# Expert loop with the down products of the former expert among gate and up, and one stretch of half-block turns

## The reference, cut to what matters

```
def expert_choice_ffn(h, router_w, w_gate, w_up, w_down):     # 16 experts, D = 1024, F = 2048, fp32
    cap = EC_CAPACITY * n // N_EXPERTS                        # 2 * 512 // 16 = 64 rows of a trunk
    aff = softmax(xf @ router_w); gate, idx = top_k(aff.T, cap)
    xs = xf[idx]
    hid = silu(xs @ w_gate[e]) * (xs @ w_up[e])               # (64, 2048)
    out = (hid @ w_down[e]) * gate[..., None]                 # (64, 1024)
    y = zeros.at[idx].add(out)
```

## Time and profile before

| | |
|---|---|
| Median of three runs | 1569.38 us (1569.37 to 1569.9) |
| Profiled execution, its time | 1570.46 us |
| Span from its first to its last instruction | 1568.7 us |
| Mean granted TensorE clock | 0.998 of full speed |
| PE busy | 1556.5 us, 99% |
| DVE busy | 1294.0 us, 82% |
| ACT busy | 1044.9 us, 67% |
| DMA from 700 to 1400 us | mean 386 GB/s |

### The profile page before, as it was taken

One profiled execution on the slowest core, in us unless ns is written; L12 is line 12 of the kernel. 1 busy time (PEld: TensorE's weight loads), 2 busy tenths in 40 slices (PEclk: granted clock), 3 DMA queues, 4 the chain that ended last, 5 costly groups with the idle time before them and its releaser, 6 DMA issues.

```text
span 1568.7 us, 22519 instructions
## 1 busy us (share of the span) xinstructions
PE 1556.5 (99%) x8254; PEld 1264.1 (81%) x8254; DVE 1294.0 (82%) x1367; ACT 1044.9 (67%) x980; POOL 160.1 (10%) x72
## 2 busy tenths in 40 slices
PE   9999999999999999999999999999999999999997
PEld 7888878888864888888888888888888888888885
DVE  7684786684864889989899998989989898998987
ACT  6453555453453777777777777777777777777776
POOL 0000000000011020211101021020202102020112
PEclk9999999999999999999999999999999999999999
DMA  9543447333465999999999999999999999999998
GB/s 338 189 145 110 142 158 259 95 122 121 155 261 219 404 399 400 392 379 388 375 389 396 379 389 379 393 378 387 395 381 389 370 398 383 389 392 379 392 358 343
DMA packets 155395, 498.41 MB, mean 318 GB/s; under 512 B 9936, under 2 KB 35664, under 8 KB 155344
## 3 DMA queue, kind: packets, MB, share of 16 engines
q1 hardware_dynamic: 144624, 461.54, 76.7%
q0 software_dynamic: 8272, 30.94, 6.2%
q10 hardware_dynamic: 2448, 5.25, 1.2%
HBM read 473.57 MB, written 20.97 MB: 315 GB/s over the span
## 4 chain that ended last, share of the span: by engine, by line
PE 96%; DVE 1%; DMA 1%; ACT 1%; SPq 0%; issue 0%; POOLq 0%; DVEq 0%
PE ps L1787 80%; PE ps L1835 4%; PE ps L1842 2%; PE ps L1926 2%; PE ps L2284 2%; PE ps L1884 1%; PE ps L1895 1%; PE ps L2090 1%; PE ps L2236 1%; PE ps L2089 1%; DMA raw<-w_qkv 1%; PE ps L2342 0%; PE ps L2085 0%; PE ps L2107 0%; DVE arena L1245 0%
## 5 line engine op out<-in xcount | busy, mean ns | idle before, releaser
L1171 DVE TENSOR_TENSOR w_rest<-raw,w_high 128x2048 fp32r<-128x2048 f32 x212 | 505.2, 2407 | 66.2 <-ACT w_high L1073 49.1
L1073 ACT CAST w_high<-raw 128x2048 fp32r<-128x2048 f32 x184 | 352.5, 1916 | 133.2 <-PE ps L1787 132.1
L1787 PE MATMUL ps<-w_high,xt_high 128*128 128x512 f32 x984 | 307.2, 392 | 0.0
L1787 PE MATMUL ps<-w_high,xt_rest 128*128 128x512 f32 x984 | 304.3, 389 | 0.0
L1787 PE MATMUL ps<-w_rest,xt_high 128*128 128x512 f32 x984 | 304.3, 389 | 0.0
L1171 DVE TENSOR_TENSOR w_rest<-raw_more,w_high 128x2048 fp32r<-128x2048 f32 x92 | 209.3, 2287 | 38.4 <-ACT w_high L1073 38.3
L1073 ACT CAST w_high<-raw_more 128x2048 fp32r<-128x2048 f32 x92 | 176.3, 1917 | 59.4 <-PE ps L1787 57.7
L1787 PEld LDWEIGHTS ps<-w_high,xt_rest 128*128 128x128 f32 x984 | 184.7, 188 | 38.5
L1787 PEld LDWEIGHTS ps<-w_rest,xt_high 128*128 128x128 f32 x984 | 184.8, 188 | 38.5
L1171 DVE TENSOR_TENSOR w_rest<-early,w_high 128x2048 fp32r<-128x2048 f32 x90 | 203.5, 2284 | 13.9 <-ACT w_high L1073 13.9
L1073 ACT CAST w_high<-early 128x2048 fp32r<-128x2048 f32 x90 | 172.5, 1917 | 59.1 <-PE ps L1787 59.1
(11 more groups left out here) (284 smaller groups left out, 1932.5 us busy)
## 6 DMA issues: line engine op xcount, KB each, us to landing
raw<-w_down SPq DMA_DIRECT2D x64, 1024.0 KB, 7.5
raw<-w_gate SPq DMA_DIRECT2D x62, 1024.0 KB, 7.4
raw<-w_up SPq DMA_DIRECT2D x62, 1024.0 KB, 7.6
raw_more<-w_down SPq DMA_DIRECT2D x32, 1024.0 KB, 7.1
early<-w_down SPq DMA_DIRECT2D x32, 1024.0 KB, 7.5
raw_more<-w_gate SPq DMA_DIRECT2D x31, 1024.0 KB
raw_more<-w_up SPq DMA_DIRECT2D x31, 1024.0 KB, 9.3
early<-w_gate SPq DMA_DIRECT2D x31, 1024.0 KB, 8.3
```

Source lines behind the costliest of these rows:

```text
L1073: nc.scalar.copy(w_high[:, i % SLOTS, :], src).then_inc(high_done, 1)
L1171: nc.vector.tensor_tensor(w_rest[:, j, :], src, w_high[:, j, :].bitcast(F32), ALU.subtract).then_inc(rest_done, 1)
L1787: done = nc.tensor.matmul(out, lhs, rhs, start=start and part == 0, stop=stop and part == 2)
```

## The change

**The loop is skewed by a whole expert.** While PE makes gate and up of expert f + 1, the down pairs of expert f stand among them. One round of the loop (f from 1 to 13) is now: gate and up, first half (pairs 8 to 15 of the round), one down pair (16), gate and up, second half (17 to 24), three down pairs (25 to 27), all three turns, then the four down pairs of the second hidden half (28 to 31). The last four continue the numbering of the next round: pair 32 is its pair 8. Expert 0 and the last two experts have their own orders, the last expert that of before.

**The turns are in half blocks.** Each 128x128 transpose becomes two, of the lower and the upper 64 rows, into the two banks of a pair of banks. A stretch is 48 transposes without a matmul between them. The rows go to banks 0 and 1, the first hidden half to 2 and 3, the second to 6 and 7: six banks. Two of these pairs belong to gate and up, so the first two pairs after the stretch wait for DVE (`xtr_done`, `htr_done`), and the second half of gate and up waits for silu and its product (`silu_done`, `hid_done`), since only one down pair lies between the halves.

**Buffers.** The two hidden halves get their own `silu` or `hid` buffer, multiplied in place (`acts`), and their own turned block: `odd_high` and `odd_rest` are new, 8 KB a partition. The copies out of PSUM read runs of 64 columns from two banks in turn (`turned`) and write in one run.

**POOL** now gathers the rows right after the turn of the former rows, and scatters a result after that.

```
+        odd_high, odd_rest = sb_line("odd_high", [P, D], F32R), sb_line("odd_rest", [P, D], F32R)
+        def turned(banks):
+            return bank(banks, 2).rearrange("p (r c t) -> p c r t", r=2, t=HD)
+        acts = (silu, hid)
+        ht = ((ht_high, ht_rest), (odd_high, odd_rest))
...
-                nc.scalar.copy(xt_high[:, :], bank(6, 2)).then_inc(xth_done, 1)
+                nc.scalar.copy(by_halves(xt_high), turned(banks)).then_inc(xth_done, 1)
...
-            def rest_of_expert(e):
-                rows_high(e + 1)
-                highs(e, 12, 12 + HT_AFTER)
-                hidden_high(2 * e + 1)
...
+            with act.Fori(1, E - 2) as f:
+                highs(f, 12, 19)
+                step_silu(2 * f + 2, pairs_before(f) + 16, 0)
+                highs(f, 19, 28)
+                step_silu(2 * f + 3, pairs_before(f) + 25, 1)
+                highs(f, 28, 31)
+                rows_high(f + 2)
+                highs(f, 31, 32)
+                hidden_high(2 * f + 2, 0, 2)
+                highs(f, 32, 36)
+                hidden_high(2 * f + 3, 1, 6, pairs_before(f) + 32)
+                result(f, pairs_before(f) + 32)
...
+            with dve.Fori(1, E - 2) as f:
+                rests(f, 12, 19)
+                step_hidden(2 * f + 2, 0)
+                rests(f, 19, 28)
+                step_hidden(2 * f + 3, 1)
+                rests(f, 28, 31)
+                rows_rest(f + 2)
+                rests(f, 31, 32)
+                hidden_rest(2 * f + 2, 0, 2)
+                rests(f, 32, 36)
+                hidden_rest(2 * f + 3, 1)
...
-                    last = nc.tensor.transpose(bank(6, 2)[:, kc * P:(kc + 1) * P], xg[:, kc * P:(kc + 1) * P], ident[:, :])
+            def turn_by_halves(c, src, banks=6):
+                for r in range(2):
+                    on = slice(r * HD, (r + 1) * HD)
+                    last = nc.tensor.transpose(bank(banks + r)[:, c * HD:(c + 1) * HD], src[on, c * P:(c + 1) * P], ident[on, on])
+                return last
+            def all_turns(e):
+                pe.wait_ge(rows_scaled, e + 1)
+                pe.wait_ge(hid_done, 2 * e + 2)
+                pe.wait_ge(htr_done, 2 * e)
+                if not isinstance(e, int):
+                    pe.nop(nofuse=True)
+                rows_t(0)
+                hidden_t(acts[0], 2)
+                hidden_t(acts[1], 6)
...
-            def rest_of_expert(e):
-                at = lambda s: lambda i: body_q(e, s + i)
-                rows_t(e + 1, 2 * e + 1)
-                pe.wait_ge(ys_done, e + 1)
-                down(2 * e, 0, at(0), 8)
-                pe.wait_ge(xtr_done, e + 3)
-                hidden_t(2 * e + 1)
-                gate_up(2 * e + 2, at(12))
-                down(2 * e + 1, 1, at(0), 20)
-                hidden_t(2 * e + 2)
+            with pe.Fori(1, E - 2) as f:
+                gate_up(f, 8, (xtr_done, f + 3), (htr_done, 2 * f + 1))
+                pe.wait_ge(ys_done, f + 1)
+                down(2 * f, 0, f, 16, 0, 1)
+                gate_up(f, 17, (silu_done, 2 * f + 3), (hid_done, 2 * f + 3))
+                down(2 * f, 0, f, 24, 1, 4)
+                all_turns(f + 1)
+                down(2 * f + 1, 1, f, 28)
```

More of the change, by code:

```diff
@@ L591, in _, with load_run @@
                 load_bias(b, GROUPS, 1)
-            def load_run(e, i, rows_of, of, h, count):
-                for jj in range(count):
+            def load_run(e, i, rows_of, of, h, end, first=0):
+                for jj in range(first, end):
                     load_pair(e, i + jj, rows_of(of, h, jj))
@@ L692, in _, with next_rows @@
             pool.wait_ge(route_done, TRUNKS)
-            for e in range(E - 1):
+            def next_rows(e):
                 pool.wait_ge(xt_mm, 2 * (e + 1))
@@ L706, in _ @@
                                         compute_op=ALU.add).then_inc(scattered, 16)
+            next_rows(0)
+            next_rows(1)
+            for e in range(2, E - 1):
+                next_rows(e)
+                scatter(e - 2)
+            scatter(E - 3)
+            scatter(E - 2)
             pool.wait_ge(rows_scaled, E - 1)
@@ L1036, in step_silu, with rows_high @@
                     return
-                nc.scalar.activation(silu, bank(0, 2), ACT.Silu).then_inc(silu_done, 1)
-            def rows_high(e):
+                nc.scalar.activation(acts[odd], bank(0, 2), ACT.Silu).then_inc(silu_done, 1)
+            def rows_high(e, banks=0):
                 if isinstance(e, int) and e == 0:
@@ L1044, in rows_high, with hidden_high @@
                 act.wait_ge(xt_mm, 2 * (e + 1))
[L1045 to L1047 removed]
+                nc.scalar.copy(by_halves(xt_high), turned(banks)).then_inc(xth_done, 1)
+            def hidden_high(s, odd, banks=6, used_by_down=None):
                 act.wait_ge(ht_mm, s + 1)
[L1049 removed]
+                if used_by_down is not None:
+                    act.wait_ge(pair_used, used_by_down)
+                nc.scalar.copy(by_halves(ht[odd][0]), turned(banks)).then_inc(hth_done, 1)
             def result(e, used_by_down):
@@ L2249, in gate_up, with down @@
                     last.then_inc(pair_used, 1)
-            def down(s, h, q_of, lo, first=0, end=D_PAIRS, lhs=(ht_high, ht_rest)):
+            def down(s, h, e, lo, first=0, end=D_PAIRS, lhs=None):
+                lhs = lhs or ht[h]
                 pe.wait_ge(htr_done, s + 1)
@@ L2272, in fourth, with hidden_t, first_hidden_t @@
                 last.then_inc(pair_used, 1)
-            def hidden_t(s, lo=0, hi=HALF // P):
-                if not isinstance(s, int):
-                    pe.wait_ge(hid_done, s + 1)
-                elif s == 0:
-                    pe.wait_ge(half_hid if lo == 0 else hid_done, 1)
-                    pe.wait_ge(third_hid_done, 1)
+            def hidden_t(src, banks=6):
+                for c in range(HALF // P):
+                    last = turn_by_halves(c, src, banks)
+                last.then_inc(ht_mm, 1)
+            def first_hidden_t(s, lo=0, hi=HALF // P):
+                pe.wait_ge(third_hid_done, 1)
+                if s == 0 and lo == 0:
+                    pe.wait_ge(half_hid, 1)
                 else:
@@ L2323, in _ @@
[L2323 to L2333 removed]
+            pe.wait_ge(rows_scaled, 1)
@@ new lines, in _ @@
+            gate_up(E - 2, 8, (xtr_done, E + 1), (htr_done, 2 * E - 3))
+            pe.wait_ge(ys_done, E - 1)
+            down(2 * E - 4, 0, E - 2, 16)
+            pe.wait_ge(hid_done, 2 * E - 1)
+            pe.wait_ge(htr_done, 2 * E - 2)
+            hidden_t(acts[0])
+            down(2 * E - 3, 1, E - 2, 20)
+            gate_up(E - 1, 0)
+            pe.wait_ge(ys_done, E)
+            down(2 * E - 2, 0, E - 1, 8, 0, 2)
+            pe.wait_ge(hid_done, 2 * E)
+            for c in range(HALF // P):
+                last = turn_whole(c, acts[1])
@@ L2334, in _ @@
+            last.then_inc(ht_mm, 1)
+            down(2 * E - 2, 0, E - 1, 8, 2, 4)
+            down(2 * E - 1, 1, E - 1, 12, 0, 2, lhs=(xt_high, xt_rest))
             pe.wait_ge(whole_done, 1)
```

170 lines of the change are left out of this document (102 added, 68 removed).

## The result

The changed kernel takes 1558.6 us (median of four runs, 1558.19 to 1558.78) against 1569.59 for the one before beside it: a ratio of 0.9928, 95% interval 0.9916 to 0.9941. That is 11.0 us less; 1558.5 had been predicted. The profiled execution took 1558.77 us with a span of 1557.0, 11.7 less than the span before.

A forecast was written before the change was run, and what follows sets the result against it. PE's own instructions were taken to bound the kernel. Fourteen stretches saving 0.78 us each give 10.9, with waits and lone turns at nothing: 1569.38 - 10.9 = 1558.5 us, range 1556.5 to 1565.

The forecast's parts named there:

- The bound: Whole loop: PE is never idle and waits for nobody, so only shortening PE's own instructions can help.
- The price of a stretch: Three turns as 48 half blocks in one stretch: 48 x 0.032 + 0.32 = 1.86 us, against 2.64 before.
- The gain: Stretches of turns, one before the loop and 13 in it: 0.78 us saved each, 14 x 0.78 = 10.9 us.
- The turns left alone: Rows of expert 1, hidden halves of experts 0 and 14: -0.05 us each, first hidden half about +0.1; together nothing.
- First rival: Last 16 transposes of a stretch come at 0.070 us, not 0.032: 1567.0 us; chance 0.10 in some degree.
- Second rival: Loads become the bound, unable to give the 1.2% more an expert wants: nothing gained, 1569.4 us; chance 0.05.
- Third rival: DVE's copies behind a stretch take 2.4 us, not 1.2; pair 12 stalls 2.1 us: 1587.9; chance 0.07 in some degree.

## Why the prediction was right

- **The bound.** That only PE's own instructions count is shown by both sides: the skewed order with whole blocks has the time of before, though every wait, buffer and bank in it is new, and the doubled rests cost nothing as long as POOL leaves DVE room for them.
- **The price of a stretch.** Predicted 1.86 us, measured 1.83. I had split one row of 32 into pace and fixed part by the length shown for it, 0.032 and 0.32. The lengths of 16, 48 and 96 give 0.031 and 0.34 to 0.37 without that. The two small errors go in opposite directions; for 48 blocks they nearly cancel.
- **The gain.** 0.78 us a round predicted, 0.82 measured, 14 times. The span fell by 11.7, the medians by 11.0, where 10.9 was predicted. That the median hits the forecast to 0.1 us is luck: the runs of one kernel differ by 0.5 to 0.6.
- **The turns left alone** were costed at 0.83 and measure 0.85 (the last of them, from 1490.35 to 1492.11, less 0.91), as the stretches of 16 in two experiments do. The half-block turn in the old order, 1 us in all instead of 2.3, is where this shows.
- **First rival, a slower pace beyond 32.** False: 96 come as 32 do. So the two figures of the Trainium skill (page TensorE: Matmul & The Clock Gate) that I had weighed for it, the queue of 64 in its table of the engine and the 62 ns where firmware decodes (section "Wait — 56ns, not 53.3ns?"), set no pace here: the 96 blocks took 31 ns each, weight loads included.
- **Second rival, the loads.** False: the round is 1.2% shorter and in the loop none of PE, DVE and ACT waits for a load of weights; from 700 to 1400 us they move 390 GB/s.
- **Third rival, dearer copies.** The copies cost what plain ones do. Its mechanism is real: doubled rests stall PE at pair 12, the place named, and a little at pair 9, which I had not named. Its size was off: I had 1.5 us of margin and a stall of 2.1, the run shows 2.1 and 1.2. POOL's multiply came 7.4 us behind the stretch and not 10, since its gather took 1.5 us to issue and not 2.8 and the data then came 1.5 us sooner. So it fell on the rest of pair 9 and not on those of 10 and 11, and held DVE up by 2.0, not 1.8; DVE swallowed a part of the doubled copies in idle time.
- **Wrong in detail.** I took a one-sided block at 0.070 us from a row of eight and concluded that two sides overlap to less than half of it. A long one-sided stretch takes 0.063, two sides in turn 0.031: 48 blocks of one side and 96 of two take the same 3.19 us. And the expectation of 1585 for one side first was wrong because I had thought the overlap needs neighbours; it reaches over some three blocks at each change of side.

Where the gain comes from, then: two halves on one side cost 0.126 us, a whole block 0.109, two halves on two sides 0.062. The overlap alone makes half blocks cheaper, by 8 x 0.047 = 0.38 us a turn, and the 0.34 to 0.37 us of entering and leaving it eat that unless three turns share them. Where these 0.35 us fall can be read from PE's starts around a stretch of the changed kernel: the first block comes 0.54 us after the last two matmuls and not 0.45 (0.09 more), the first matmul behind comes 1.63 us after the first block and not 48 x 0.031 = 1.49 (0.14 more), and its successor but one after 0.57 and not 0.45 (0.12 more). Why PE takes this time at the change between the two kinds isn't shown.

## What to carry to other kernels

Read a mode's price at two lengths, as a fixed part and a pace: here the fixed part (about 0.35 us) was as large as what one turn could win, so the same transposes gained 1 us in 45 places and 11 us in 14. When work is regrouped to share such a part, the price is paid in waits elsewhere; list for each the time at which it is wanted and the time at which it is ready, and look which other engine's work falls into the gap (here POOL's multiply, whose 2 us cost nothing alone and 1.2 us a round once three more copies stood beside it). A gain on an engine that never waits can be added up from its timeline to the microsecond.

## What of the hardware I had not expected

A transpose of 64 rows by 128 columns in fp32 takes 0.063 us in a stretch of its own side and 0.031 where the sides alternate, so the second side is free. (Only the lower side was run alone.) The same 48 blocks last 1.70 us with sides in turn, 2.23 sorted by eight and 3.00 sorted by 24. DVE and POOL waited for each other's whole instruction, and the profile shows the wait as a longer instruction: 4.29 us for a rest of 2.28, 2.08 us for a multiply of 8 columns. And the stretches of 48 and 96 transposes left the granted clock at 1.00 (2.4 GHz) in every window above.
